# PEER expert stage on one core: 32 tokens more taken out of the first expert matmuls, longer routing stretches, marks by eight tokens, a sixth row slot, 14 dots in the second half

## What is computed

```python
q = (xt @ wq).reshape(t_len, 8, 2, 64)
s_top, i_top = lax.top_k(sub, 16)            # sub: q against 2 x 128 subkeys, per head
sc, ci = lax.top_k(cand, 16)                 # the 16 best pairs of each of the 8 heads
eid = (i1 * 128 + i2)                        # 128 expert numbers of 16,384, for every token
gate = softmax(sc)
h = gelu(einsum('cd,ced->ce', xc, u[eid]))   # dot of the token with 128 rows of u
out = einsum('ce,ced->cd', gate * h, v[eid]) # weighted sum of 128 rows of v
```

## Time and profile before

| what | value |
|---|---|
| median of 3 runs | 1729.89 us (1728.78 to 1734.46) |
| the profiled execution | 1732.18 us, span 1730.4 us |
| TensorE busy | 1689.1 us, 98% |
| VectorE busy | 1255.8 us, 73% |
| ScalarE busy | 768.7 us, 44% |
| GpSimd busy | 820.7 us, 47% |
| moved by DMA | 417.65 MB, 241 GB/s over the span |

### The profile page before, as it was taken

One profiled execution on the slowest core, in us unless ns is written; L12 is line 12 of the kernel. 1 busy time (PEld: TensorE's weight loads), 2 busy tenths in 40 slices (PEclk: granted clock), 3 DMA queues, 4 the chain that ended last, 5 costly groups with the idle time before them and its releaser, 6 DMA issues.

```text
span 1730.4 us, 24570 instructions
## 1 busy us (share of the span) xinstructions
PE 1689.1 (98%) x9061; PEld 1486.3 (86%) x9061; DVE 1255.8 (73%) x2490; ACT 768.7 (44%) x1301; POOL 820.7 (47%) x496
## 2 busy tenths in 40 slices
PE   7999999999999999999999999999999999999997
PEld 6667767778878999999999999999888888888886
DVE  2487896562353778789888987534888888888886
ACT  4444444522232443775577367534333333333332
POOL 5222222344446466766777677776433232332312
PEclk9999999999999999999999999999999999999998
...
GB/s 200 61 62 50 59 60 54 77 94 146 84 112 110 113 197 186 306 372 345 253 333 384 249 286 386 383 364 296 405 390 354 384 376 351 383 372 354 389 190 85
DMA packets 126360, 417.65 MB, mean 241 GB/s; under 512 B 12961, under 2 KB 32417, under 8 KB 124705
## 3 DMA queue, kind: packets, MB, share of 16 engines
...
...
## 4 chain that ended last, share of the span: by engine, by line
PE 88%; DVE 8%; ACT 2%; issue 1%; DMA 1%; POOL 0%; SPq 0%; another core or an unknown queue 0%; ACTq 0%; DVEq 0%; POOLq 0%
PE ps L1285 16%; PE ps L1287 16%; PE ps L1286 16%; PE ps L1514 11%; PE ps L1511 11%; PE ps L1512 11%; PE ps L1609 5%; PE ps L1370 1%; DVE dist_a L842 1%; DVE row L895 1%; DVE row L866 1%; DVE small L841 1%; PE ps L1395 1%; DVE small L892 1%; DMA raw<-w_units 0%
## 5 line engine op out<-in xcount | busy, mean ns | idle before, releaser
L1285 PE MATMUL ps<-tok_hi,w_hi 128*128 128x384 f32 (+2 forms) x1544 | 548.8, 355 | 8.4 <-issue 3.6
L1287 PE MATMUL ps<-tok_hi,w_lo 128*128 128x384 f32 (+2 forms) x1544 | 539.3, 349 | 0.0
L1286 PE MATMUL ps<-tok_lo,w_hi 128*128 128x384 f32 (+2 forms) x1544 | 539.3, 349 | 0.0
L539 ACT ACTIVATE w_hi<-raw 128x1024 fp32r<-128x1024 f32 x334 | 353.3, 1058 | 414.0 <-PE ps L1514 301.4
L486 POOL TENSOR_TENSOR w_lo<-raw,w_hi 128x1024 fp32r<-128x1024 f32 x128 | 318.2, 2489 | 165.8 <-ACT w_hi L539 165.2
L439 POOL TENSOR_TENSOR w_lo<-raw,w_hi 128x1024 fp32r<-128x1024 f32 x80 | 195.0, 2442 | 327.0 <-ACT w_hi L539 326.8
L1285 PEld LDWEIGHTS ps<-tok_hi,w_hi 128*128 128x128 f32 x1544 | 291.1, 189 | 35.7 <-issue 10.2
L1287 PEld LDWEIGHTS ps<-tok_hi,w_lo 128*128 128x128 f32 x1544 | 290.8, 188 | 18.6
L1286 PEld LDWEIGHTS ps<-tok_lo,w_hi 128*128 128x128 f32 x1544 | 291.3, 189 | 16.8
L1511 PE MATMUL ps<-w_hi,gh_hi 128*128 128x512 f32 x768 | 298.8, 389 | 0.0
L1512 PE MATMUL ps<-w_lo,gh_hi 128*128 128x512 f32 x768 | 298.8, 389 | 0.0
...
## 6 DMA issues: line engine op xcount, KB each, us to landing
raw<-u_units SPq DMA_DIRECT2D x128, 512.0 KB
raw<-v_rows SPq DMA_DIRECT2D x128, 512.0 KB
...
gelu_d<-gelu_t ACTq DMA_DIRECT2D x120, 192.0 KB
...
```

The lines of the kernel that those rows point to most:

```text
L539: act.activation(w_hi[:, n % RAW, :], raw[:, n % RAW, :], ACT.Copy).then_inc(hi_done, 1)
L1285: pe.matmul(out_, l_hi, r_hi, start=start, stop=False)
L1286: pe.matmul(out_, l_hi, r_lo, start=False, stop=False)
L1287: return pe.matmul(out_, l_lo, r_hi, start=False, stop=stop)
```

## The change

Tokens 128 to 159 (NEAR = 32) leave the dense u matmuls: an expert unit multiplies 352 columns (UT) instead of 384. Their 32 x 128 dots are made like those of the first tile, with 32 more gathers and dots (DOTS = 160): the 128 partitions hold the 32 tokens four times, once for each of four groups of expert ranks, so one gather fetches four ranks of each token. `keep_near` copies the picks of tile 1, four small DMAs spread the expert numbers, four the token rows, four bring the gelus back, and `weigh_near` multiplies them into the gates. The gelu buffer of these tokens is set to 1, so the value half is unchanged in size. The quads of these tokens are done last, after a second turn of picks (`turn_picks(4)`) inside the last mark stretch.

The order is 14 first units, routing stretches of 19, mark stretches of 13, 17 and 21 units with 24, 32 and 40 quads, and 6 units in the tail. Dots: 8, 10, 10 in routing (in six groups), 30, 36, 46 in the mark stretches, 6 in the tail and 14 in the first value units. A compare covers eight tokens (128x1024). A sixth slot for rows of u is used from the end of the second routing to the middle of the last mark stretch. One value weight in four has its lower part made on GpSimd (`by_pool`). The fmas run from unit 11 to unit 118. In the value half three token tiles use other PSUM banks (`ffn_bank`: 2, 4, 0).

```diff
-FIRST_UNITS, ROUTE_UNITS, MARK_UNITS = 16, 14, 16
-TAIL = FIRST_UNITS + 3 * (ROUTE_UNITS + MARK_UNITS)
-ROUTE_DOTS, MARK_DOTS = (3, 6, 6), 30
-U_SLOTS, V_SLOTS = 5, 6
-FMA_START, FMA_END = 2, P - 12
+NEAR = 1 * TOK
+UT = DT - NEAR
+NEAR_GROUPS = P // NEAR
+DOTS = P + NEAR
+FIRST_UNITS, ROUTE_UNITS, MARK_UNITS = 14, 19, (13, 17, 21)
+TAIL = FIRST_UNITS + 3 * ROUTE_UNITS + sum(MARK_UNITS)
+ROUTE_DOTS, MARK_DOTS, TAIL_DOTS, LATE_DOTS = (8, 10, 10), (30, 36, 46), 6, 14
+NEAR_FROM, NEAR_END = 50, 50 + NEAR
+assert sum(ROUTE_DOTS) + sum(MARK_DOTS) + TAIL_DOTS + LATE_DOTS == DOTS
+U_SLOTS, V_SLOTS = 6, 6
+FMA_START, FMA_END = LATE_DOTS * 2 // 3 + 2, P - 10
...
+def quads_of(b, k):
+
+    first, count = first_quad(b), first_quad(b + 1) - first_quad(b)
+    return range(first + count * k // MARK_UNITS[b - 1], first + count * (k + 1) // MARK_UNITS[b - 1])
+
+
+def pairs_of(b, k):
+
+    return [q for q in quads_of(b, k) if q % 2 == 0]
+
+
+def stretch_dots():
+
+    by = [0] * FIRST_UNITS
+    for b in range(1, NT):
+        for units, dots in ((ROUTE_UNITS, ROUTE_DOTS[b - 1]), (MARK_UNITS[b - 1], MARK_DOTS[b - 1])):
+            by += [by[-1] + dots * (k + 1) // units for k in range(units)]
+    units = P - TAIL
+    return by + [by[-1] + TAIL_DOTS * (k + 1) // units for k in range(units)]
+
+
+DOTS_BY = stretch_dots()
+NEAR_UNIT = next(k for k in range(P) if DOTS_BY[k] >= NEAR_END) + 3
...
+def slots_at(d):
+
+    return 3 if d < ROUTE_DOTS[0] else U_SLOTS if SIX_FROM <= d < SIX_END else U_SLOTS - 1
...
+def fmas_by(j):
+
+    return max(0, min(P, P * (j - FMA_START + 1) // (FMA_END - FMA_START)))
+
+
+def late_dots_by(j):
+
+    return min(DOTS, DOTS - LATE_DOTS + 3 * (j + 1) // 2)
+
+
+DOT_SLOTS = dot_slots()
+
+
+def by_pool(j):
+
+    return j + LO_AHEAD < P and j % 4 == 1
...
+                j = n - first - P
+                if by_pool(j):
+                    engine.wait_ge(lo_pool, P + sum(by_pool(i) for i in range(j + 1)))
+                else:
+                    engine.wait_ge(lo_dve, sum(not by_pool(i) for i in range(j + 1)))
...
-                if j == P - 8:
-                    sp.wait_ge(gate_read, N_QUAD)
-                    for s in range(2):
-                        sp.wait_ge(stage_out[s], 16 * (NB // 2))
-                    load_gates(0, 0)
-                if j == P - 4:
-                    load_gates(0, 1)
+            sp.wait_ge(gate_read, N_QUAD)
+            for s in range(2):
+                sp.wait_ge(stage_out[s], 16 * (NB // 2))
+            load_gates(0, 0)
             for j in range(P):
                 load_unit(U_VAL + j, v_rows[:, (j - KEPT) % P, :])
+                if j == 1:
+                    load_gates(0, 1)
...
-            rows_to(P)
+            sent = 0
+            for j in range(P):
+                if by_pool(j):
+                    expert_lo(P + j)
+                rows_to(late_dots_by(j) + U_SLOTS - 1)
+                while sent < min(P, fmas_by(j - 1) + V_SLOTS):
+                    get_v(sent)
+                    sent += 1
...
-                    act.activation(gelu_t[:, j % 2, :], ps[:, j % 2, 0:DT], ACT.Gelu).then_inc(bank_read, 1)
+                    act.activation(gelu_t[:, j % 2, :], ps[:, j % 2, 0:UT], ACT.Gelu).then_inc(bank_read, 1)
...
+            def spread_near_eid():
+
+                act.wait_ge(near_set, 1)
+                for g in range(NEAR_GROUPS):
+                    part = slice(NEAR * g, NEAR * g + NEAR)
+                    act.dma_start(near_eid[part, :], near_all[0:NEAR, part]).then_inc(near_eid_in, 16)
...
+            def finish_near():
+
+                act.wait_ge(dot_done, NEAR_END)
+                act.activation(near_dot[:], near_dot[:], ACT.Gelu).then_inc(near_gelu, 1)
+                act.wait_ge(near_gelu, 1)
...
+            def keep_near():
+
+                dve.wait_ge(pick_set, 2)
+                dve.scalar_tensor_tensor(near_all[:], pick[:, 0, :], float(NK), pick[:, 1, :], ALU.mult, ALU.add)\
+                    .then_inc(near_set, 1)
+                dve.tensor_copy(near_keys[:], pick[:, 0:2, :])
+                settled(dve.tensor_copy(near_gate[:], pick[:, 2, :]))
+
+            def weigh_near():
+
+                dve.wait_ge(near_h_in, 16 * NEAR_GROUPS)
+                dve.tensor_tensor(near_gate[0:NEAR, :], near_gate[0:NEAR, :], near_h[0:NEAR, :], ALU.mult)\
+                    .then_inc(near_pick, 1)
...
-                s, quad = q % 4, q % 32
+                b, quad = tile_quad(q)
                 if q >= 4:
-                    dve.wait_ge(gate_full, q - 3)
-                first, second, gate = (ps[:, 5, a * P + 4 * quad:a * P + 4 * quad + 4].unsqueeze(2).to_broadcast([P, 4, P])
-                                       for a in range(3))
-                numbers = iota[:].unsqueeze(1).to_broadcast([P, 4, P])
-                dve.tensor_tensor(left[:, s, :, :], numbers, first, ALU.is_equal)
-                dve.tensor_tensor(match[:, s, :, :], numbers, second, ALU.is_equal).then_inc(match_set, 1)
-                if right_by(q)[0] == "dve":
-                    dve.wait_ge(match_set, q + 1)
-                    dve.tensor_tensor(right[:, s, :, :], match[:, s, :, :], gate, ALU.mult).then_inc(right_dve, 1)
+                    dve.wait_ge(gate_full, q - 2)
+                first, second = (ps[:, 5, a * P + 4 * quad:a * P + 4 * quad + 8].unsqueeze(2).to_broadcast([P, 8, P])
+                                 for a in range(2))
+                numbers = iota[:].unsqueeze(1).to_broadcast([P, 8, P])
+                two = slice(q % 4, q % 4 + 2)
+                dve.tensor_tensor(left[:, two, :, :].rearrange("p s t k -> p (s t) k"), numbers, first, ALU.is_equal)
+                dve.tensor_tensor(match[:, two, :, :].rearrange("p s t k -> p (s t) k"), numbers, second, ALU.is_equal)\
+                    .then_inc(match_set, 1)
+                if right_by(q + 1)[0] == "dve":
+                    gate = ps[:, 5, 2 * P + 4 * quad + 4:2 * P + 4 * quad + 8].unsqueeze(2).to_broadcast([P, 4, P])
+                    dve.wait_ge(match_set, q // 2 + 1)
+                    dve.tensor_tensor(right[:, 3, :, :], match[:, 3, :, :], gate, ALU.mult).then_inc(right_dve, 1)
...
+                parts = iter([before + ROUTE_DOTS[b - 1] * i // 6 for i in range(1, 7)])
                 route(b, lambda: dots_to(next(parts)))
+                if b == 1:
+                    keep_near()
                 spread_picks(b)
-                for k in range(MARK_UNITS):
-                    for quad in (2 * k, 2 * k + 1):
-                        mark(32 * (b - 1) + quad)
-                    dots_to(dots_by(routed_at(b) + ROUTE_UNITS + k))
+                for k in range(MARK_UNITS[b - 1]):
+                    for quad in pairs_of(b, k):
+                        if b == NT - 1 and tile_quad(quad) == (NT, 0):
+                            weigh_near()
+                            spread_picks(NT)
+                        mark(quad)
+                    dots_to(DOTS_BY[routed_at(b) + ROUTE_UNITS + k])
...
-                if j + LO_AHEAD < P:
+                if j + LO_AHEAD < P and not by_pool(j):
                     value_lo(j)
                 if j + 3 < P:
                     times_gelu(j + 3)
-                if j >= FMA_START:
-                    fmas_to(P * (j - FMA_START + 1) // (FMA_END - FMA_START))
+                dots_to(late_dots_by(j))
+                fmas_to(fmas_by(j))
...
-                tokens = slice(P, S) if n >= U_EXP else slice(0, S)
-                to = ps[:, bank, 0:DT] if n >= U_EXP else ps[:, bank, :]
+                tokens = slice(P + NEAR, S) if n >= U_EXP else slice(0, S)
+                to = ps[:, bank, 0:UT] if n >= U_EXP else ps[:, bank, :]
...
-                pe.wait_ge(pick_set, b + 1)
+                if b == NT:
+                    pe.wait_ge(near_pick, 1)
+                    pe.wait_ge(match_set, (N_QUAD - NEAR // 4) // 2)
+                    pe.wait_ge(right_dve, (N_QUAD - NEAR // 4) // 4)
+                    pe.wait_ge(gate_full, N_QUAD - NEAR // 4)
+                else:
+                    pe.wait_ge(pick_set, b + 1)
                 for k in range(3):
-                    last = pe.transpose(ps[:, 5, k * P:(k + 1) * P], pick[:, k, :], ident[:])
+                    picked = pick[:, k, :] if b < NT else near_keys[:, k, :] if k < 2 else near_gate[:]
+                    last = pe.transpose(ps[:, 5, k * P:(k + 1) * P], picked, ident[:])
...
+                    for quad in quads_of(b, k):
+                        if b == NT - 1 and tile_quad(quad) == (NT, 0):
+                            turn_picks(NT)
+                        gates_of(quad)
...
+                    if j == 0 and t == NT - 1:
+                        pe.wait_ge(bank_read, BANK_EXP + P)
```

207 lines of the change are left out of this document (137 added, 70 removed).

## The result

The changed kernel takes **1765.18 us** (median of 4 runs, 1761.73 to 1766.46) where the kernel before takes 1731.26 beside it: a ratio of **1.0196**, 95% interval 1.0177 to 1.0216. It is slower by 34 us, clear of the noise; the forecast was 1716. The profiled execution has a span of 1764.6 us against 1730.4.

What follows compares the result with a forecast made beforehand. It took TensorE, 88% of the chain and without gaps, as the bound: -40.9 + 8 + 4.5 + 7.1 + 4.5 + 3 = -13.8 us, hence 1716 us. It gave 8 in 10 to 1697 to 1735.

Steps and rivals of the forecast that it cites:

- Routing: Routing stretches: VectorE's routing with ten dots, 60.9 us and some 3 more, fits TensorE's 73 us; cost 0.
- The mark stretches: Mark stretches, 281.4 us of TensorE work: VectorE 92% busy, DMA asked for 394 GB/s; +8 us (0 to 19).
- a sign of being wrong: Mark stretches: the forecast is wrong if together they exceed 281 us by more than 20.
- The turn of picks: Last mark stretch: the second turn stands right before a dependent quad with no unit between; +4.5 us (4 to 6).
- From experts to values: Last gates (T0) to first value matmul: gate store and loads outlast the six units; +7.1 us (1.9 to 20.1).
- GpSimd ... +4.5: Fourth value unit: its weight's lower part is queued on GpSimd behind rows; +4.5 us (0 to 8).
- late dots +3: First value units: more rows of u per unit go through full queues; +3 us (0 to 8).
- -40.9: Expert matmuls: 352 columns at 0.160 us instead of 384 at 0.1733 save 40.9 us.
- Rival (c): DMA engines become the bound at about 370 GB/s: marks +19, handover +20.1; slower, 1745 us; chance 0.15.
- Rival (b): Gain spent at the handover, where the gate store takes 13.2 us; marks +14, crowding +8; 1731 us; chance 0.17.
- (a): The feed holds everywhere: marks at no cost, store in 5.2 us, no crowding; 1700 us; chance 0.16.
- (d): Expert units: the narrow matmul is not faster and most waits stay; some 1740 us; chance 0.02.

Runs made afterwards that it cites:

- e1_six_late: The changed kernel with only the sixth slot for rows of u taken up six rows later: 1748.28 us, 1.0102 of the kernel before.
- c2_six_as_changed: c2_late20 with the sixth slot taken from the row at which the changed kernel takes it: 1729.98 us, 0.9985 of the kernel before.
- c2_late20: c1_mended with the near picks turned one unit earlier, six fewer mark dots, twenty late dots begun later, rows of v later: 1715.89 us.
- c1_mended: The changed kernel with four orders mended (sixth slot, first value loads, half gate group, GpSimd's first value low part): 1739.2 us.

## Why the prediction was wrong

- **"Routing ... Cost 0; the cover is 9 us or more."** This is the step whose mechanism failed. It compared VectorE's work with the stretch, and by itself that comparison held (e1_six_late: no gap over 2 us in the second or the third routing). But I did not follow the sixth slot's wait on GpSimd. The change adds `wait_ge(pick_set, 3)` to the gather of one row; the row is asked for five dots ahead, in the routing whose end it waits for, and experts' low parts are queued behind. Measured: 16.7 us lost in that stretch, 17 in time (e1_six_late), 12.5 with the other waits mended (c2_six_as_changed). The third routing lost 4.1 more, 3.86 of it a gap before its transposes, with VectorE busy 85.5 of 87 us; with the slot mended that gap is gone too. The Trainium skill (Perfetto Trace Analysis, Tensor Engine Instruction (MATMUL, LD_WEIGHTS)) says that GpSimd, like VectorE and ScalarE, is a strict first-in, first-out queue. The trace agrees: two low parts start only behind the gather that waited 19.53 us.
- **"The mark stretches ... +8"**, with "+4.5" for the second turn: 12.5 forecast, 37.7 measured (14.4, 6.7, 16.6), in number the largest miss. The stretches took 85.3 + 99.9 + 132.5 = 317.7 us, 36 above the 281.4 needed, beyond the 20 that the prediction itself gave as a sign of being wrong; they moved 351, 379 and 346 GB/s where it wanted 390. VectorE at 92% fits (91% in the first marks with no row to wait for). What was mis-sized is the feed of rows. I set 394 GB/s asked against 407 held; in the first marks the engines moved 351 at 0.93, so they were not full there. 30 rows in 13 units had to go through five slots: I added a sixth slot to the sum that does not exist yet in the first marks. Four slots instead of five took the rate from 348 to 322 GB/s and cost 10 us. The second marks did reach 409 GB/s for 41 us, with TensorE busy 40.75 of them. So a test of the DMA rate alone was the wrong test for the first marks. For the third marks, at 346 GB/s and 16.6 us, the cause beyond late rows stays open. The Trainium skill (HBM Reference, Specifications) has 358 GB/s as a core's share: exceeded here again, with 409, by one core running alone.
- **The turn of picks**: a gap of 3.95 us and 3.78 - 1.78 = 2.0 of slow gates, against 4.5 forecast: 6.0 us, right as a place and at the top of its bounds (4 to 6). Removed, it gave nothing that the time shows.
- **"From experts to values +7.1"**: the store landed near T0 + 15.5 (1199.19), forecast 14.4. Then the two halves took until VectorE's first product at 1216.44, T0 + 32.7, where I had 26.2: 17.2 us for 4.19 MB and not 11.8; and from there 5.9 us to the first value matmul, not 4.0, since the first gh_low took 2.57 us and not 0.55. And I left ScalarE out: its wait for the first value load held an expert unit up. The start slipped 15.7 us (38.7 against 23.0), inside the forecast's 1.9 to 20.1.
- **"GpSimd ... +4.5"**: a gap of 3.49 us at the fourth value unit, released by GpSimd's low part. Right. With this, "late dots +3" and the start, 14.6 were forecast and 24.4 measured. Three gaps are 16.5 of it, the rest slow matmuls. No gap stands behind the fourth value unit, where the late dots were priced.
- **"-40.9"**: 0.160 was a straight line; the rows show 0.158 and 0.167. The term is 46.1 at best and 20 at worst. In the changed kernel, with 480 long steps, it was 42.
- **A term that was missing**: the cost behind a gap. I priced each wait by its length. Half-speed matmuls and the longer distance (4.0) add 27.8 us to 55.0 of gaps.
- **The sum**: the forecast had +27.1 beside the -40.9, the trace has +81.7 beside -46.1. Rival (c) forecast a slower kernel by the DMA engines as the bound, 1745. Its sign was right, but that was not its mechanism: other orders, with the same 431.06 MB still moved, took off 49 us, and (c) too put the routing at nothing. A share of the DMA engines in the marks is not ruled out; leaving out the near rows was tried only in c2_late20, where little was left to win. Rival (b) priced the handover at 11.3 + 4.5 + 8 = 23.8, close to the 24.4 measured, but the marks at 14 + 4.5 and the routing at nothing, and so gave 1731. Rivals (a) and (d) fall.

How the 49 us from 1765 to 1716 divide is not fully settled: 17 and 7 were measured alone, both with two smaller ones gave 26. Between c1_mended and c2_late20 lie 23 us by the times and 25 by the spans of the profiled executions. By the account these are the first marks (17.4 to 5.3 us), the third routing (3.8 to 0.0), the third marks (13.5 to 7.8) and the handover (16.4 to 11.6); 3.5 us of the whole, net, is the distance of 0.158 in place of 0.167, to which the third routing's part is due, and belongs to no mend.
